# Six products of a gate slab moved ahead of a program boundary, and the key norm placed earlier, in a hybrid recurrent decoder step

## The reference, cut to what matters

```python
def token_mixer(h, ...):
    proj = h @ w_in[l]
    p_ret, p_gla, p_rwkv, p_merge = split_cols(proj, ...)
    y_ret, sr = retention_branch(p_ret, ...)
    y_gla, sg = gla_branch(p_gla, ...)
    y_rw, sw, ss = rwkv7_branch(p_rwkv, ...)
    gates = sigmoid(p_merge).reshape(B, T, 3, 1024)
    merged = (gates[:, :, 0] * (y_ret @ wb[0]) + gates[:, :, 1] * (y_gla @ wb[1])
              + gates[:, :, 2] * (y_rw @ wb[2]))
    out = merged @ w_out[l]

def rwkv7_branch(...):          # the part of it that the change touches
    a = sigmoid(a0 + ad @ a_up)
    kk = hs(k * kk_scale)
    kk = kk * rsqrt(sum(kk * kk, axis=-1, keepdims=True) + 1e-12)
    ...
    y = y + sum(r_h * k_h * rk, axis=-1, keepdims=True) * v_h
```

## Time and profile before

| | |
|---|---|
| median of 3 runs | 2766.46 us (2762.11 to 2770.38) |
| profiled execution, own time | 2763.13 us |
| its span | 2761.3 us |
| TensorE busy | 2646.6 us, 96% of the span |
| TensorE weight loads busy (beside the matmuls) | 2156.1 us, 78% |
| VectorE busy | 841.2 us, 30% |
| ScalarE busy | 572.1 us, 21% |
| mean granted TensorE clock | 0.985 |

### The profile page before, as it was taken

One profiled execution on the slowest core, in us unless ns is written; L12 is line 12 of the kernel. 1 busy time (PEld: TensorE's weight loads), 2 busy tenths in 40 slices (PEclk: granted clock), 3 DMA queues, 4 the chain that ended last, 5 costly groups with the idle time before them and its releaser, 6 DMA issues. The chain is left out here.

```text
span 2761.3 us, 78487 instructions
## 1 busy us (share of the span) xinstructions
PE 2646.6 (96%) x34890; PEld 2156.1 (78%) x34890; DVE 841.2 (30%) x2467; ACT 572.1 (21%) x1736; POOL 0.2 (0%) x4
## 2 busy tenths in 40 slices
PE   8999999999899999999999999989799999999998
PEld 5777877777677777677787777767699999999987
DVE  2023665556411000202366555541311111110111
ACT  2223333332200000122333233320111111111011
POOL 0000000000000000000000000000000000000000
PEclk9999999999999999999999999999799999999999
DMA  6333432222243433333443222224399999999995
GB/s 217 107 124 139 157 124 76 69 75 69 79 136 125 135 132 126 123 96 124 148 153 123 73 69 76 75 87 137 108 375 389 354 356 381 380 355 367 377 340 229
DMA packets 144459, 495.94 MB, mean 180 GB/s; under 512 B 18608, under 2 KB 23344, under 8 KB 141648
## 3 DMA queue, kind: packets, MB, share of 16 engines
q1 hardware_dynamic: 144208, 492.23, 49.8%
HBM read 471.88 MB, written 20.29 MB: 178 GB/s over the span
## 5 line engine op out<-in xcount | busy, mean ns | idle before, releaser
L384 PEld LDWEIGHTS psum<-work,ring 128*64 128x64 f32 x16896 | 648.1, 137 | 37.3 <-issue 23.4
L384 PE MATMUL psum<-work,ring 128*64 128x88 f32 x16896 | 664.4, 240 | 10.2 <-issue 9.0
L293 PE MATMUL psum<-hT,ring 128*128 128x288 f32 x2048 | 555.1, 413 | 0.0
L293 PEld LDWEIGHTS psum<-hT,ring 128*128 128x128 f32 x2048 | 372.2, 191 | 93.9 <-ACT work L395 2.7
L377 PE MATMUL psum<-hT,ring 128*128 128x288 f32 x768 | 187.1, 406 | 0.0
L1412 ACT ACTIVATE work<-psum 128x256 f32<-128x256 f32 (+4 forms) x304 | 102.5, 370 | 394.4 <-PE psum L1327 98.8
L377 PEld LDWEIGHTS psum<-hT,ring 128*128 128x128 f32 x768 | 145.8, 190 | 40.9 <-issue 0.8
L1819 PE MATMUL psum<-hT,ring 128*128 128x288 f32 x704 | 172.6, 409 | 1.7 <-DVE hT L1893 1.7
L1819 PEld LDWEIGHTS psum<-hT,ring 128*128 128x128 f32 x704 | 134.7, 192 | 39.6 <-issue 2.1
L2418 DVE TENSOR_TENSOR work<-psum,work 128x88 f32<-128x88 f32 x176 | 43.8, 249 | 354.0 <-PE psum L384 342.6
L2406 DVE TENSOR_TENSOR xT<-xT,psum 128x288 f32<-128x288 f32 x64 | 29.1, 454 | 317.2 <-PE psum L2288 317.2
(11 more groups left out here) (404 smaller groups left out, 2963.7 us busy)
## 6 DMA issues: line engine op xcount, KB each, us to landing
ring<-w_ff_dram SPq DMA_DIRECT2D x540, 512.0 KB, 6.5
ring<-w_mix_dram SPq DMA_DIRECT2D x256, 512.0 KB, 3.7
ring<-w_ff_dram SPq DMA_DIRECT2D x72, 384.0 KB, 7.2
work<-s_gla_dram SPq DMA_DIRECT2D x8, 1024.0 KB, 5.4
gla_s_out<-work SPq DMA_DIRECT2D x8, 1024.0 KB, 4.6
work<-s_ret_dram SPq DMA_DIRECT2D x8, 512.0 KB, 4.7
ret_s_out<-work SPq DMA_DIRECT2D x8, 512.0 KB, 3.1
work<-s_rw_dram SPq DMA_DIRECT2D x16, 256.0 KB, 2.5
```

The costliest lines, as they stand in the source:

```text
L293: mm = nc.tensor.matmul(out, ring[:, s, k, :], rhs[:, k, :], start=(k == 0), stop=(k == KT - 1))
L384: mm = nc.tensor.matmul(out[64 * c:64 * c + 64], ring[:, s, k, 64 * c:64 * c + 64], rhs[:, k0 + k, :], start=(k0 + k == 0), stop=(k0 + k = ...
```

## The change

The first six of the eight products of the first gate slab (i = 0, j = 0) are made at the end of `gated_linear`, behind `square_sum(GLA_H - 1)`, into bank 6, with the group of accumulation left open (`stop=False`); TensorE waits there for the slab and for `row` to reach 25, which says that slab 22 has left bank 6. The generator `side` starts that slab with its seventh product. In the prologue the calls `side(8)`, `side(8)`, `side(16)` become `side(6)`, `side(6)`, `side(14)`. Both layers run this code. The number of products is the same, and so is every load. All lines behind the insertions are numbered 1 or 5 higher in the changed kernel (line 293 becomes 294, 1131 becomes 1136).

```diff
 RING = 8
+SIDE_BEGUN = 6
 WORK = 16032
@@ class Between
-        def __init__(self, slabs):
-            self.products = self.emit(slabs)
-
-        def emit(self, slabs):
-            for wait, s, out, rhs in slabs:
+        def __init__(self, slabs, begun=0):
+            self.products = self.emit(slabs, begun)
+
+        def emit(self, slabs, begun):
+            for n, (wait, s, out, rhs) in enumerate(slabs):
                 wait()
-                for k in range(KT):
+                for k in range(begun if n == 0 else 0, KT):
                     mm = nc.tensor.matmul(out, ring[:, s, k, :], rhs[:, k, :], start=(k == 0), stop=(k == KT - 1))
@@ gated_linear, TensorE
             square_sum(GLA_H - 1)
+            slab_arrived(pe, S_SIDE, 0, 0)
+            pe.wait_ge(sig("row"), GLA_H * 6 + 1)
+            for n in range(SIDE_BEGUN):
+                mm(B[6][:, 0:T], ring[:, 0, n, :], hT[:, n, :], start=(n == 0), stop=False)
@@ rwkv, TensorE
             side = Between([(lambda i=i, j=j: side_wait(i, j), j, SIDE_BANK[j % 2][:, 0:T], (hT, hT, y_ret, y_gla)[j])
-                            for i in range(KT) for j in range(4)])
+                            for i in range(KT) for j in range(4)], begun=SIDE_BEGUN)
@@
             lora_up(0)
-            side(8)
+            side(6)
             key_norm(0)
-            side(8)
+            side(6)
             bonus_sum(0)
-            side(16)
+            side(14)
             scores(0)
```

## The result

| | before | after |
|---|---|---|
| median of 6 runs each | 2767.26 us | 2749.97 us |
| lowest to highest | 2762.11 to 2770.38 | 2748.38 to 2752.43 |
| profiled execution, own time | 2763.13 us | 2751.98 us |
| its span | 2761.3 us | 2750.2 us |
| mean granted TensorE clock | 0.985 | 0.988 |

The ratio is 0.994, with an interval of 0.9928 to 0.9953: 0.6% faster, 17.3 us between the medians. The forecast was 7.7 us. So the medians put the gain at 12 to 17 us. The two profiles alone differ by 11.1 us.

A forecast was written before the change was run, and what follows sets the result against it. TensorE, busy in 96% of the span, bounds the kernel. Two layers of 2.90 - 0.10 - 0.49 give 4.6 us, the clock 3.1: -7.7 us, 2759.0 against the median 2766.46, range 2754 to 2764.5.

The forecast's parts named there:

- What bounds the kernel, and the room for the six products: TensorE, busy in 96% of the span; six products, 2.90 us a layer, fit its 2.9 us free before the meeting.
- The meeting, -0.1: Where gated branch and delta rule meet: TensorE reports at 414.45 where the last engine did at 414.4, losing 0.1 us.
- The rival that TensorE comes late: At the meeting TensorE holds everybody up by 0.5 us a layer, gates' wait takes 0.8: 2763.3 us; chance 0.08.
- The wait for the gates, -0.49: In the prologue, the bonus sum's two records leave the wait for the gates' sigmoids and return as waiting, 0.49 us.
- the key norm, 0: In the prologue, VectorE's square is ready at 418.53, TensorE arrives at 420.0: no wait, the move costs nothing by itself.
- The clock, two thirds of 4.6: Behind both meetings: the shorter pause saves two thirds of the half-speed start's 2.24 and 2.39 us, 3.1 us together.
- "never falls": Rival: the clock never falls at either meeting, so its whole loss is won: -9.2 us, 2757.3 us; chance 0.2.
- Rows 8: Profile rows with lone pauses of 1.43, 1.55 and 1.70 us, granted clock 1.00 throughout; taken as favouring a clock that holds.
- Rows 9 and 10: Profile rows with pauses of 1.51 and 1.71 us, 0.75 us of work between, then clock 0.51 for 3.5 us.
- lora_up's first record of 0.81 us: Behind the meeting, 0.81 us against 0.51 in rows 6: hardly fills the engine, which could count as more idleness.
- The loop gets the same products at the same points, so it is only shifted: Behind the prologue, the loop's filler keeps its places and the loop only moves in time; no term in the sum.
- the slower rival: Shifting adds half-speed stretches behind layer 0's meeting, 1.7 us each; six give 2772 us; chance 0.05.

The follow-up runs named there:

- k1: The changed kernel again with no edit, as control for later runs on its chip: 2752.05 us, 0.9961 of the kernel before.
- i1: Changed kernel with the bonus sum back in the wait for the gates and throwaway products in TensorE's two pauses between the layers: 2748.57 us, ratio 0.9945.
- j0: Changed kernel with both last steps filled with throwaway products, run again as control: 2754.52 us, 0.9955 of the kernel before.
- j1: Changed kernel with both last steps filled, plus five throwaway products ahead of layer 1's first scores: 2755.35 us, 0.9959 of the kernel before.
- e0: The changed kernel again with no edit, beside the kernel before on the same chip: 2750.29 us, ratio 0.9953.
- e1: Kernel before, with six products made ahead of the meeting and thrown away, the prologue still making all 32: 2762.13 us, ratio 0.9985.
- e3: Changed kernel with the bonus sum put back four filler products behind the key norm, then 16: 2750.77 us, 0.9952 of the kernel before.
- h2: Kernel before with three throwaway products (1.45 us) ahead of layer 1's first scores: 2766.45 us, ratio 1.001.
- h1: Changed kernel with five throwaway products (2.4 us) ahead of layer 1's first scores: 2759.07 us, 0.9974 of the kernel before.
- f1: Kernel before with one throwaway product at each of 17 places in the loop's last step where filler has run out: 2762.87 us, ratio 0.9991.
- f2: Changed kernel with one throwaway product at each of 17 places in the loop's last step: 2752.33 us, 0.9949 of the kernel before.
- g1: Changed kernel with five throwaway products (2.4 us) ahead of layer 0's first scores only: 2753.92 us, 0.9955 of the kernel before.

## Why the prediction was wrong

**What bounds the kernel, and the room for the six products.** Right: 2.9 us of free time ahead of the meeting, and 12 records without a gap in it.

**The meeting, -0.1.** TensorE came at 414.1 together with the others, and it cost nothing. The rival that TensorE comes late is out.

**The wait for the gates, -0.49, and the key norm, 0.** Right: one wait of 0.80 us where 0.32 were, and none at the key norm or the scores. VectorE's chain was ready 3.4 us before the scores (427.61 + 0.45 against 431.46).

**The clock, two thirds of 4.6.** Mis-sized: at both meetings the clock held in full, 2.24 and 2.39 us, as the rival "never falls" had it (the first in the list, which the prediction elsewhere calls the second). Its 9.2 us for the meetings stand beside 9.4 measured. Rows 8 were the ones to go by. Rows 9 and 10 have two such pauses with only 0.75 us of work between them, which this place hasn't; and even there the clock doesn't always fall. It fell in 13 of the 17 profiles and held in k1, i1, j0 and j1, with the same pauses. Here is k1, against the earlier trace rows:

```profile
836.63 0.75 PE L1814 MATMUL psum<-work,table 128*128 128x288 f32 x2 [1.51 <-DVE work L1881]
839.10 6.30 PE L1824 MATMUL psum<-hT,ring 128*128 128x288 f32 x25 [1.71 <-DVE hT L1898]
...
839.00:843.00 4.00, 3.90 (x16) 3.14 (x17) 2.95 (x7) 0.70 (x1) 0.00 (x0) 1.00 0.00 0
```

The prediction also took lora_up's first record of 0.81 us, against 0.51 in rows 6, for a sign that it hardly fills the engine; that was the half-speed clock itself, and behind the short pause the record takes 0.48. By the Trainium skill, "TensorE: Matmul & The Clock Gate", Part 1, a pause like this should have left the clock alone, and here the trace agrees, at both meetings and in e0, e1 and e3 as well.

**The step that failed** is "The loop gets the same products at the same points, so it is only shifted", together with the sentence in the slower rival that a shift has no preferred direction. The part is in the kernel before's own trace, and I had priced it (1.7 us for a stretch like rows 10) as a risk that averages out, and put it at nothing in the sum. It isn't nothing: the last step of each layer takes 31.5 to 38.1 us by where the clock falls in it, the change's runs have some 11 us less at half speed outside the meetings than those of before, worth about 3 us, and a shift of 2.4 us in layer 1 cost 6 to 7 us. That term and the clock's mis-sized one are both in favour. With all of 9.4 us from the meetings and 3 from the last steps the result would have been 2767.26 - 12.4 = 2754.9, just inside the range; the 5 us more in this comparison than that are not assigned (12.1 and 15.0 us in the two repeats against 17.3 here), so part of the miss looks like scatter, and that the sum moved out of the range this way and not back into it is then luck. I also took the three runs' scatter of 8 us for noise of the measurement; filling the last steps halved the scatter, so much of it was this.

**The reference point.** The profiled execution of before lay 3.3 us under the median of its three runs, 4.1 under that of six; the profiled one of the changed kernel lay 2.0 above its median. The sum of -7.7 was made against the first.

**What stays open.** Why the change's last steps are at full speed more often. One profile a kernel shows where the last steps fell, not how often they do; the map from them misplaced h2 and k1. That the term comes from the last steps alone rests on the filled pair on one chip and on h1 with j0 and j1. Nor is the 10.5 us between the filled kernels split further than 9.4 and 1.1, and the expert part scatters by some us between executions (1.3 us less in the profile after).

## What to carry to other kernels

A pause of TensorE can cost twice: its own time, and a half-speed stretch behind it (at the pauses of 4.1 to 4.3 us here, not at those of 1.4). Before pricing a move of work into a pause, read the granted clock for the microseconds behind the pause; here that was nearly as much as the moved work itself (2.24 us beside 2.41), and throwaway products won it too. And read the clock wherever TensorE is busy for only part of the time, as in the last step here (69 to 76%): such a stretch can run at either clock, from one execution to the next and from one edit ahead of it to the next; a few per mille of gain or loss that no edited line explains may be that, and a variant of both kernels with that stretch filled, and the mean clock over many runs, tell the two apart.

## What the runs showed of the hardware

- At half speed the same step of the same instructions took 38.1 us instead of 31.5 to 32.0, with TensorE busy for 17.5 of 23.0 us (76%) and the clock at 0.51 throughout (e1, h1); in other executions the same work at 69% busy held 1.00 (e0). That so full a stretch can stay at half speed for 23 us I had not expected.
- Products in a pause cost nothing measurable as long as they ended with the other engines (line 815: 12 records, and the meeting 0.02 and 0.05 us longer), and where TensorE's pauses were shorter than the product, 17 of them cost 3 us (34.7 against 31.5 to 32.0, f1 and f2).
- The same two pauses of 1.5 and 1.7 us in `mix_out`, 0.75 us of work apart, were followed by half speed in 13 profiles and by full speed in 4.
- Adding 2.4 us of work cost 1.9 to 3.6 us in layer 0 (g1, against the change on other chips) and 6 to 7 us in layer 1 (h1, on one chip).
